# Layer boundaries of a two-block transformer kernel on one core: order of low parts, high parts, squares and additions, and idle matrix products between layers

## The chip, the cores and the metric

The kernel runs on one core of one Trainium2 chip. The metric is the device time of one execution in microseconds (us). The core has five engines that matter here: TensorE (PE) for matrix products, VectorE (DVE), ScalarE (ACT), GpSimd (POOL), and SyncE (SP), which issues the loads. Each engine runs its own list of instructions in order and waits on semaphores that the others raise.

## The reference

The input x is 512 tokens by 1024 features. A first block and then a stack of four mixer layers are applied, every one with a residual and an RMS norm. What matters here is the pattern between two layers:

```
y = xf * lax.rsqrt(jnp.mean(xf * xf, axis=-1, keepdims=True) + EPS)      # rms_norm, times a gain
...
h = h + 0.5 * rms_norm(f, g_ffn1_post[i])
u = rms_norm(h, g_mix_pre[i])
qkv = u @ w_in[i]
...
h = h + rms_norm(mixed @ w_out[i], g_mix_post[i])
f = swiglu(rms_norm(h, g_ffn2_pre[i]), w_ffn2_gate[i], w_ffn2_up[i], w_ffn2_down[i])
h = h + 0.5 * rms_norm(f, g_ffn2_post[i])
e = (p[i] @ w_ple_proj[i]) * jax.nn.sigmoid(h @ w_ple_gate[i])
h = h + rms_norm(e, g_ple_post[i])
```

Four times, then, the output F of a layer is normalized, scaled by a gain and added to h, and the new h is normalized and multiplied by the next layer's weights. All of it is in float32.

## The kernel before

**Layout.** h, F, and the split input of a product are held transposed: 8 blocks (DB = 8) of 128 features by 512 tokens. A float32 product is made of three products of fp32r parts: x is split in a high part xh (ACT) and a low part xl = x − xh (DVE), a weight tile in wh (ACT) and wl (DVE), and TensorE adds xh·wh, xl·wh and xh·wl (`mm3`, lines 320 to 322). A stage of the table `stages` is a row of weight tiles of 1024 by 128; SP loads them four ahead.

**A layer boundary** is what this case is about. At the end of a layer, `post_out` (or the code of the stage ple) squares F block by block on ACT and adds the squares up on POOL (`sum_squares`: a copy for block 0, L459, then additions into `acc`, L462). TensorE sums over the features with products against ones (`sums_pe`, L344: first of `acc`, then of the last square), DVE and ACT make the inverse root, and TensorE spreads it over the partitions (`spread_pe`, L366). Then a new `Block` begins, and `Prologue` runs, with `update` set at four boundaries: into mix_in, ffn2_up, ple and conv_in. Its work for the 8 blocks b is dealt out like this:

- DVE (`Prologue.dve`): F[b] is scaled by the inverse root, read from a PSUM bank, and the gain (L415); for even b the sum h[b] = F[b] + h[b] (L419); the low part xl[b] (L437; L434 in ple, which has no gain), placed two blocks behind the scaling.
- POOL (`Prologue.pool`, `sum_squares`): the sum h[b] for odd b (`add`, L450), and the running sum of the new squares. Before square b is added, for even b, `add(b + 1)` is called.
- ACT (`Prologue.act`): the high part xh[b] (L401), then the square of h[b] into one of two buffers (L405), which from b = 2 on waits until POOL has added square b − 2.
- PE (`pe_tiles`, `head_mm`): the first three tiles of a stage (HEAD = 3) are multiplied together, block by block, so that TensorE can start when block 0 is ready. A block takes six products that need xh[b] (L469, L470) and three that need xl[b] (L473). Behind the head come the sums over squares (`sums_pe`), and, inside the next tile, `spread_pe`.

The stage ple has no squares in its prologue (its input is not normalized); there ACT also copies the products of p and splits weights between the blocks, and DVE splits two weight tiles ahead of its steps 3 and 5. `keep_busy` issues products of constants (ident by ones) whose result nobody reads; before the change it is used around the end of the first block's attention and at the start of mix_out (L1653, L1738, L1749, L1756).

The order within an engine is the order in which the code is written; no scheduler changes it.

Of the kernel before, what the change touches and what calls it, by code (L numbers as in the profile page):

```python
# [29 lines left out]
ACT = mybir.ActivationFunctionType  # L30
# [4 lines left out]
DB = D // P  # L35
# [19 lines left out]
def kernel_program(nc, I, out):  # L55
    top = ExitStack()
    with top:
# [133 lines left out]
        h = sb("h", [P, DB, SEQ])  # L191
# [182 lines left out]
        class Prologue:  # L374
# [17 lines left out]
            def act(self, act, after=()):  # L392

                after = dict(after)
                for b in range(DB):
                    if b in after:
                        after[b](act)
                    if self.update is not None:
                        act.wait_ge(h_pool if b % 2 else h_new, self.h0 + b // 2 + 1)
                    g = 1.0 if self.gain is None else self.gain[:, b:b + 1]  # L400
                    nc.scalar.activation(xh[:, b, :], h[:, b, :], ACT.Copy, scale=g).then_inc(xs_hi, 1)  # L401
                    if self.squares:
                        if b >= 2:
                            act.wait_ge(acc_done, self.acc0 + b - 1)
                        nc.scalar.activation(sq[:, b % 2, :], h[:, b, :], ACT.Square).then_inc(sq_done, 1)  # L405

            def dve(self, dve, after=()):
                after = dict(after)
                for b in range(DB):
                    if b in after:  # L410
                        after[b](dve)
                    if self.update is not None:
                        if b == 0:
                            dve.wait_ge(spread, self.root + 1)
                        nc.vector.scalar_tensor_tensor(out=F[:, b, :], in0=F[:, b, :], scalar=self.update[:, b:b + 1],  # L415
                                                       in1=ps[STAT][:, :], op0=ALU.mult, op1=ALU.mult).then_inc(f_scaled, 1)
                        if b % 2 == 0:
                            dve.wait_ge(f_scaled, self.fs0 + b + 1)
                            nc.vector.tensor_tensor(h[:, b, :], F[:, b, :], h[:, b, :], ALU.add).then_inc(h_new, 1)  # L419
                        if b >= 2:  # L420
                            self.low(dve, b - 2)
                    else:
                        self.low(dve, b)
                if self.update is not None:
                    self.low(dve, DB - 2)
                    self.low(dve, DB - 1)

            def high(self, act, b):
# [23 lines left out]
        def sum_squares(pool, sq0, acc0, add=None):  # L452

            for b in range(DB - 1):
                if add is not None and b % 2 == 0:
                    add(pool, b + 1)
                pool.wait_ge(sq_done, sq0 + b + 1)
                if b == 0:
                    nc.gpsimd.tensor_copy(acc[:, :], sq[:, 0, :]).then_inc(acc_done, 1)  # L459
                else:  # L460
                    pool.wait_ge(acc_done, acc0 + b)
                    nc.gpsimd.tensor_tensor(acc[:, :], acc[:, :], sq[:, b % 2, :], ALU.add).then_inc(acc_done, 1)  # L462
# [33 lines left out]
            return 4 + j if isinstance(i, int) and i == 1 and j < 2 else j  # L496

        def pe_tiles(pe, name, x_hi, x_lo, ev0, x_ready=None, parts=1, sums=None, at=None,
                     beside=None, loop_end=None, x_pe=None, amid=None, bank_of=None, x_at=None, joined=None, frees=False, held=False):

            def body(i, j):
                r, s, kb, t, got = tile_at(name, i, j, 0)
                o, bank, part = output_of(i, j, parts)
                if amid is not None:
                    bank = two_banks(o)  # L510
                if bank_of is not None:
                    bank = bank_of(i, j)
                first_i = isinstance(i, int) and i == 0
                if first_i and x_ready is not None and j < HEAD:
                    if j:
                        return
                    pe.wait_ge(lo_done, t + HEAD)
                    if joined is not None or held:
                        pe.wait_ge(evac, ev0 - 1)
                    for b in range(kb):  # L520
                        if joined is not None and b == 2:
                            sums_pe(pe, *joined)
                        if at is not None and sums is None and b == 4:
                            spread_pe(pe, at)
                        if x_pe is not None:
                            x_pe(pe, b)
                        head_mm(pe, range(HEAD), t, b, x_ready, x_hi, x_lo)
                    if sums is not None:
                        sums_pe(pe, *sums)
                    return  # L530
                pe.wait_ge(lo_done, t + 1)
                if part == 0 and bank < 4:
                    wait(pe, evac, ev0 + o - (3 if amid is None or first_i or o in (4, 5) else 1))
                for b in range(kb):
                    if first_i and j == HEAD and b == 2 and sums is not None:
                        spread_pe(pe, at)
                    xb = part * WB + b
                    if x_at is not None and o == 0 and (b == 0 or xb >= FB - 4):
                        pe.wait_ge(*x_at(max(xb, min(part * WB + kb, FB - 4) - 1)))
                    last = mm3(pe, ps[bank][:, :], s, b, x_hi[:, xb, :], x_lo[:, xb, :],  # L540
                               xb == 0, part == parts - 1 and b == kb - 1)
                    if b == kb - 1:
                        last.then_inc(tile_done, 1)
                    elif frees and o == DB - 1:
                        last.then_inc(x_free, 1)
                    if amid is not None:
                        amid(pe, o, b)
                if beside is not None and isinstance(i, int):
                    beside(pe, 4 * i + j)
            steps(pe, name, body, loop_end, 2 if bank_of is ffn_bank else 1)  # L550


        def in_proj(name, gain, dst, update=None, sums=None, tails=(), evac_dve=None, evac_act=None, loop_end=None,
# [13 lines left out]
            with ExitStack() as own:  # L567
# [81 lines left out]
                @block.tensor  # L649
                def _(pe):  # L650
                    pe_tiles(pe, name, xh, xl, ev0, x_ready=pro.x0, sums=None if joined else pro.sums, at=st, joined=sums,
                             beside=beside.get("pe"), loop_end=loop_end, amid=beside.get("pe_amid"))
                    if "pe" in tails:
                        tails["pe"](pe, ev0)
            return ev0
# [14 lines left out]
        at = 0  # L670
# [113 lines left out]
        def ffn_up(block, name, gain, update, act_hi, act_lo, sp_end=None, boot=None, pool_start=None):  # L784
# [75 lines left out]

            @block.tensor
            def _(pe):
                pe_tiles(pe, name, xh, xl, ev0, x_ready=pro.x0, sums=pro.sums, at=st, bank_of=ffn_bank)
            return ev0


# [5 lines left out]
        def post_out(block, name, x_hi, x_lo, parts=1, x=None, x_at=None, amid=None, between=(None, None)):  # L872
# [51 lines left out]
            @block.tensor  # L924
            def _(pe):
                pe_tiles(pe, name, x_hi, x_lo, ev0, x_ready=x_ready, parts=parts, x_pe=x_pe, x_at=x_at,
                         bank_of=None if x_at is None else down_bank, beside=None if amid is None else amid["pe"])
                sums_pe(pe, acc0 + DB - 1, sq0 + DB, between[0])
                if between[1] is not None:
                    between[1](pe)  # L930
                spread_pe(pe, st)


# [912 lines left out]
        with ExitStack() as c:  # L1846
# [10 lines left out]
            with nc.Block() as block:  # L1857
# [66 lines left out]
                @block.tensor  # L1924
                def _(pe):
                    for o in range(2, DB):
                        p_product(pe, o)
                    t = t0 + PACKED
                    pe.wait_ge(lo_done, t + HEAD)
                    for b in range(DB):  # L1930
                        head_mm(pe, range(HEAD), t, b, pro.x0, xh, xl)
                    for o in range(HEAD, DB):
                        s = (t + o) % SPLIT
                        pe.wait_ge(lo_done, t + o + 1)
                        wait(pe, evac, ev0 + o - 3 if o > 3 else 0)
                        for b in range(DB):
                            last = mm3(pe, ps[o % 4][:, :], s, b, xh[:, b, :], xl[:, b, :], b == 0, b == DB - 1)
                        last.then_inc(tile_done, 1)
                    sums_pe(pe, acc0 + DB - 1, sq0 + DB)
                    spread_pe(pe, st)  # L1940

        ple_ctx.close()

        with ExitStack() as c:
# [14 lines left out]
            with nc.Block() as block:  # L1959
# [64 lines left out]

                @block.tensor
                def _(pe):
                    pe_tiles(pe, name, xh, xl, ev0, x_ready=pro.x0, sums=pro.sums, at=st)

            joint = ExitStack()
            sums, block, pro = resid_out("conv_out", *split_x(lambda b: yall[:, b, :]),  # L2030
# [1121 lines left out]
```

## Time and profile before

| | |
|---|---|
| median of 3 runs | 2263.16 us (2261.5 to 2265.85) |
| the profiled execution's own time | 2260.62 us |
| its span in the trace | 2258.9 us |
| TensorE matmul busy | 2174.8 us, 96% of the span |
| VectorE busy | 1132.9 us, 50% |
| ScalarE busy | 869.1 us, 38% |
| GpSimd busy | 409.6 us, 18% |
| granted TensorE clock, mean | 0.98 of full |
| loads | 182.14 MB, mean 81 GB/s |

Shares are of the whole span. TensorE is nearly always at work, so a time on another engine costs only where TensorE waits for it. Those places are few and short, and the four layer boundaries with an update hold a good part of them. The granted clock is either full (2.4 GHz) or half (1.2 GHz). Starts are in us from the span's start.

### The profile page before, as it was taken

To read this page: it belongs to the slowest core of one execution; us is meant where nothing else is said; L and a number is where in the kernel's file an instruction comes from. 1 tells how busy PE (TensorE), PEld (TensorE's weight loads), DVE (VectorE), ACT (ScalarE), POOL (GpSimd) and SP (SyncE) were. 2 spreads that over 40 slices of the span, in tenths; PEclk is the share of its full clock that TensorE was granted. 3 is DMA by queue.
4 is the path that set the end of the run, shared out by engine and by line. 5 is a ranking of instruction groups with operands and counts; after the bars stand their busy time and mean duration, and the time that the engine had idled before them with its cause. 6 is when DMAs were issued, how large, how long until landed. Compare 5 with 4: busy or idle time off the path is not lost. (4 is left out here: it accounts for less than half of the span.)

```text
span 2258.9 us, 29190 instructions
## 1 busy us (share of the span) xinstructions
PE 2174.8 (96%) x10874; PEld 1760.1 (78%) x10874; DVE 1132.9 (50%) x1801; ACT 869.1 (38%) x1426; POOL 409.6 (18%) x450
## 2 busy tenths in 40 slices
PE   8999999999999999999899999999999999999998
PEld 6888887766677888888778877887788887886667
DVE  5444323544445444322575544336556777665444
ACT  4322223554434322223432233225446753443353
POOL 2111001213313111100230011001110242014441
PEclk9999999999999999999999999999999998999999
DMA  4333333511022333332233346860143221243111
GB/s 144 110 95 100 96 99 84 101 56 56 20 75 57 112 102 93 105 93 76 81 93 102 93 68 96 109 92 20 39 131 89 63 56 39 66 98 75 47 48 47
DMA packets 359323, 182.14 MB, mean 81 GB/s; under 512 B 41925, under 2 KB 356014, under 8 KB 358830
## 3 DMA queue, kind: packets, MB, share of 16 engines
q1 hardware_dynamic: 358872, 180.57, 32.4%
q8 instruction: 69, 1.13, 0.2%
q14 instruction: 40, 0.33, 0.1%
q10 hardware_dynamic: 342, 0.12, 0.0%
HBM read 176.14 MB, written 4.52 MB: 80 GB/s over the span
## 5 line engine op out<-in xcount | busy, mean ns | idle before, releaser
L320 PE MATMUL ps<-xh,wh 128*128 128x512 f32 x1912 | 760.7, 398 | 1.4 <-DVE wl L287 1.4
L322 PE MATMUL ps<-xh,wl 128*128 128x512 f32 x1912 | 745.6, 390 | 0.0
L321 PE MATMUL ps<-xl,wh 128*128 128x512 f32 x1912 | 744.6, 389 | 0.0
L287 DVE TENSOR_TENSOR wl<-raw,wh 128x1024 fp32r<-128x1024 f32 x328 | 417.9, 1274 | 416.4 <-ACT wh L277 412.1
L277 ACT ACTIVATE wh<-raw 128x1024 fp32r<-128x1024 f32 x328 | 341.2, 1043 | 359.2 <-PE ps L322 313.9
L320 PEld LDWEIGHTS ps<-xh,wh 128*128 128x128 f32 x1912 | 359.1, 188 | 83.7 <-issue 10.8
L322 PEld LDWEIGHTS ps<-xh,wl 128*128 128x128 f32 x1912 | 358.9, 188 | 76.6
L321 PEld LDWEIGHTS ps<-xl,wh 128*128 128x128 f32 x1912 | 359.4, 188 | 73.2 <-issue 2.4
L469 PE MATMUL ps<-xh,wh 128*128 128x512 f32 x312 | 129.6, 416 | 25.4 <-DVE wl L287 10.9
L462 POOL TENSOR_TENSOR acc<-acc,sq 128x512 f32<-128x512 f32 x72 | 102.9, 1430 | 263.4 <-ACT sq L904 178.9
L320 PE MATMUL ps<-a_hi,wh 128*128 128x512 f32 x352 | 137.0, 389 | 0.0
L322 PE MATMUL ps<-a_hi,wl 128*128 128x512 f32 x352 | 137.0, 389 | 0.0
L321 PE MATMUL ps<-a_lo,wh 128*128 128x512 f32 x352 | 136.9, 389 | 0.0
L815 POOL TENSOR_TENSOR F<-F,rstd 128x512 f32<-128x512 f32 x44 | 57.1, 1298 | 397.9 <-ACT F L831 397.9
L470 PE MATMUL ps<-xh,wl 128*128 128x512 f32 x312 | 127.0, 407 | 0.0
L473 PE MATMUL ps<-xl,wh 128*128 128x512 f32 x312 | 92.8, 407 | 2.4 <-DVE xl L437 2.4
L469 PEld LDWEIGHTS ps<-xh,wh 128*128 128x128 f32 x312 | 62.2, 199 | 41.7 <-issue 15.5
L834 ACT ACTIVATE a_hi<-ps 128x512 f32 (+1 forms) x44 | 26.3, 598 | 163.3 <-DVE ps L855 163.3
L459 POOL COPY acc<-sq 128x512 f32<-128x512 f32 x12 | 8.9, 739 | 424.1 <-ACT sq L974 318.0
L831 ACT ACTIVATE F<-ps 128x512 f32<-128x512 f32 x44 | 26.3, 599 | 149.6 <-DVE ps L852 149.6
L321 PEld LDWEIGHTS ps<-a_lo,wh 128*128 128x128 f32 x352 | 66.1, 188 | 13.7
L320 PEld LDWEIGHTS ps<-a_hi,wh 128*128 128x128 f32 x352 | 66.1, 188 | 13.7
(397 smaller groups left out, 2564.3 us busy)
## 6 DMA issues: line engine op xcount, KB each, us to landing
raw<-in_w_ffn_gate SPq DMA_DIRECT2D x44, 512.0 KB, 3.8
raw<-in_w_ffn_up SPq DMA_DIRECT2D x44, 512.0 KB, 3.7
raw<-in_w_ffn_down SPq DMA_DIRECT2D x32, 512.0 KB, 3.9
raw<-in_conv_w_in SPq DMA_DIRECT2D x32, 512.0 KB, 4.1
raw<-in_fox_w_in SPq DMA_DIRECT2D x32, 512.0 KB, 10.5
raw<-in_gdn_w_in SPq DMA_DIRECT2D x32, 512.0 KB, 4.1
raw<-in_w_in SPq DMA_DIRECT2D x24, 512.0 KB, 3.8
raw<-in_swa_w_in SPq DMA_DIRECT2D x32, 256.0 KB, 3.8
```

Of the source, the lines that this page charges most:

```text
L277: nc.scalar.activation(wh[s][:, 0:kb, :], raw[r][:, 0:kb, :], ACT.Copy).then_inc(hi_done, 1)
L287: nc.vector.tensor_tensor(wl[s][:, 0:kb, :], raw[r][:, 0:kb, :], wh[s][:, 0:kb, :].bitcast(F32), ALU.subtract).then_inc(lo_done, 1)
L320: pe.matmul(o, wh[s][:, kb, :], x_hi, start=start, stop=False)
L321: pe.matmul(o, wh[s][:, kb, :], x_lo, start=False, stop=False)
L322: return pe.matmul(o, wl[s][:, kb, :], x_hi, start=False, stop=stop)
L462: nc.gpsimd.tensor_tensor(acc[:, :], acc[:, :], sq[:, b % 2, :], ALU.add).then_inc(acc_done, 1)
L469: pe.matmul(ps[g][:, :], wh[s][:, b, :], x_hi[:, b, :], start=b == 0, stop=False)
L470: pe.matmul(ps[g][:, :], wl[s][:, b, :], x_hi[:, b, :], start=False, stop=False)
L473: last = pe.matmul(ps[g][:, :], wh[(t + g) % SPLIT][:, b, :], x_lo[:, b, :], start=False, stop=b == DB - 1)
L815: nc.gpsimd.tensor_tensor(SR[:, s, :], S[:, s, :], rstd[:, :], ALU.mult).then_inc(sr_done, 1)
L831: nc.scalar.activation(S[:, s, :], ps[ffn_bank(i, j)][:, :], ACT.Silu).then_inc(silu_done, 1)
L834: nc.scalar.activation(act_hi[:, bass.ds(p, 1), :], ps[ffn_bank(i, j)][:, :].rearrange("p (o q) -> p o q", o=1), ACT.Copy).then_inc(up_hi, 1)
```

## The change

Five edits:

1. `Prologue.act`: the high part of block b + 1 now comes ahead of the square of block b.
2. `Prologue.dve`: the low part stands one block behind the scaling instead of two.
3. `sum_squares`: POOL's additions to odd blocks of h come ahead of squares 0, 1, 2 and 3, instead of 0, 2, 4 and 6.
4. Idle products: 9 ahead of the head of mix_in, ffn2_up and conv_in (a new argument `idle_bank` of `pe_tiles`), 4 between sums and spread of ffn1_down and mix_out, 8 ahead of the sums of ple and 4 between its sums and spread.
5. ffn2_down, which has products of p between its sums and its spread, gets none; the head of ple gets none either.

```diff
@@ Prologue.act
                     nc.scalar.activation(xh[:, b, :], h[:, b, :], ACT.Copy, scale=g).then_inc(xs_hi, 1)
-                    if self.squares:
-                        if b >= 2:
-                            act.wait_ge(acc_done, self.acc0 + b - 1)
-                        nc.scalar.activation(sq[:, b % 2, :], h[:, b, :], ACT.Square).then_inc(sq_done, 1)
+                    if self.squares and b >= 1:
+                        self.square(act, b - 1)
+                if self.squares:
+                    self.square(act, DB - 1)
+
+            def square(self, act, b):
+                if b >= 2:
+                    act.wait_ge(acc_done, self.acc0 + b - 1)
+                nc.scalar.activation(sq[:, b % 2, :], h[:, b, :], ACT.Square).then_inc(sq_done, 1)
@@ Prologue.dve
-                        if b >= 2:
-                            self.low(dve, b - 2)
+                        if b >= 1:
+                            self.low(dve, b - 1)
                     else:
                         self.low(dve, b)
                 if self.update is not None:
-                    self.low(dve, DB - 2)
                     self.low(dve, DB - 1)
@@ sum_squares
             for b in range(DB - 1):
-                if add is not None and b % 2 == 0:
-                    add(pool, b + 1)
+                if add is not None and b < DB // 2:
+                    add(pool, 2 * b + 1)
                 pool.wait_ge(sq_done, sq0 + b + 1)
@@ pe_tiles
+                    if idle_bank is not None:
+                        keep_busy(pe, idle_bank, 9)
                     pe.wait_ge(lo_done, t + HEAD)
@@ in_proj (mix_in) and ffn_up (ffn2_up); conv_in passes idle_bank=6
+                             idle_bank=None if update is None else 6)
@@ post_out
                 if between[1] is not None:
                     between[1](pe)
+                else:
+                    keep_busy(pe, 6, 4)
                 spread_pe(pe, st)
@@ ple
+                    keep_busy(pe, 4, 8)
                     sums_pe(pe, acc0 + DB - 1, sq0 + DB)
+                    keep_busy(pe, 4, 4)
                     spread_pe(pe, st)
```

**POOL at the start of conv_in.** Names are destination, then sources; `h<-F,h` is the addition to an odd block, `acc<-sq` and `acc<-acc,sq` the running sum of squares. Before:

```order
L450 TENSOR_TENSOR h<-F,h 128x512 [waits f_scaled]
L459 COPY acc<-sq 128x512 [waits sq_done]
L462 TENSOR_TENSOR acc<-acc,sq 128x512 [waits acc_done,sq_done]
L450 TENSOR_TENSOR h<-F,h 128x512 [waits f_scaled]
L462 TENSOR_TENSOR acc<-acc,sq 128x512 [waits acc_done,sq_done] x2
L450 TENSOR_TENSOR h<-F,h 128x512 [waits f_scaled]
L462 TENSOR_TENSOR acc<-acc,sq 128x512 [waits acc_done,sq_done] x2
L450 TENSOR_TENSOR h<-F,h 128x512 [waits f_scaled]
L462 TENSOR_TENSOR acc<-acc,sq 128x512 [waits acc_done,sq_done]
```

Now:

```order
L454 TENSOR_TENSOR h<-F,h 128x512 [waits f_scaled]
L463 COPY acc<-sq 128x512 [waits sq_done]
L454 TENSOR_TENSOR h<-F,h 128x512 [waits f_scaled]
L466 TENSOR_TENSOR acc<-acc,sq 128x512 [waits acc_done,sq_done]
L454 TENSOR_TENSOR h<-F,h 128x512 [waits f_scaled]
L466 TENSOR_TENSOR acc<-acc,sq 128x512 [waits acc_done,sq_done]
L454 TENSOR_TENSOR h<-F,h 128x512 [waits f_scaled]
L466 TENSOR_TENSOR acc<-acc,sq 128x512 [waits acc_done,sq_done] x4
```

Behind the addition to block 7, which waits for DVE's last scaling, there stood one addition of a square; now there stand four.

**ACT at the start of conv_in**, from the high part of block 5 on (`xh<-h,vA`, with its square `sq<-h`). Before:

```order
L401 ACTIVATE xh<-h,vA 128x512 [waits h_new_pool]
L405 ACTIVATE sq<-h 128x512 [waits acc_done]
L401 ACTIVATE xh<-h,vA 128x512 [waits h_new]
L405 ACTIVATE sq<-h 128x512 [waits acc_done]
L401 ACTIVATE xh<-h,vA 128x512 [waits h_new_pool]
L405 ACTIVATE sq<-h 128x512 [waits acc_done]
L277 ACTIVATE wh<-raw 128x1024 [waits tile_done,loaded1]
```

Now:

```order
L401 ACTIVATE xh<-h,vA 128x512 [waits h_new_pool]
L410 ACTIVATE sq<-h 128x512 [waits acc_done]
L401 ACTIVATE xh<-h,vA 128x512 [waits h_new]
L410 ACTIVATE sq<-h 128x512 [waits acc_done]
L401 ACTIVATE xh<-h,vA 128x512 [waits h_new_pool]
L410 ACTIVATE sq<-h 128x512 [waits acc_done] x2
L277 ACTIVATE wh<-raw 128x1024 [waits tile_done,loaded1]
```

The squares between the high parts of blocks 5, 6 and 7 were those of 5 and 6; they are now those of 4 and 5, and the squares of 6 and 7 stand together behind the last high part.

**PE between ple and conv_in** (`ps<-ones,ident` is an idle product) in the kernel after:

```order
L485 MATMUL ps<-ones,ident 128x128 x8
L344 MATMUL ps<-ones,acc 128x1 x4
L344 MATMUL ps<-ones,sq 128x1 x4
L485 MATMUL ps<-ones,ident 128x128 x4
L366 MATMUL ps<-ident,rms_col 128x128 x4
L1867 UNCONDITIONAL_BRANCH
L2037 UNCONDITIONAL_BRANCH
L485 MATMUL ps<-ones,ident 128x128 x9
L473 MATMUL ps<-xh,wh 128x512
```

The three rows of L485 are new; the rest stood there in the same order.

## Rows read from the trace of the kernel before

**Rows 1.** The page, part 1: busy us (share) xinstructions of each engine.

```profile
PE 2174.8 (96%) x10874; PEld 1760.1 (78%) x10874; DVE 1132.9 (50%) x1801; ACT 869.1 (38%) x1426; POOL 409.6 (18%) x450
```

**Rows 2.** Waits of PE, whole span: us in total, times, longest.

```profile
PE ps L469 <- ACT xh L401: 8.1, 3, 2.7
...
PE ps L366 <- ACT rms_col L360: 2.8, 3, 1.0
...
PE ps L344 <- POOL acc L462: 2.5, 1, 2.5
```

**Rows 3.** Stretches: length, busy us (instructions) by engine, granted clock, DMA share, GB/s.

```profile
385.15:409.28 24.13, 21.32 (x89) 17.07 (x90) 21.20 (x21) 10.57 (x17) 17.61 (x13) 0.86 0.62 110
694.76:718.90 24.14, 20.48 (x89) 16.19 (x90) 21.21 (x21) 10.56 (x17) 16.98 (x11) 0.89 0.30 79
1133.93:1158.01 24.08, 21.03 (x89) 16.55 (x90) 21.19 (x21) 10.57 (x17) 17.06 (x13) 0.86 0.29 76
...
1130.40:1140.60 10.20, 6.60 (x20) 4.92 (x21) 7.11 (x12) 3.83 (x7) 4.26 (x6) 0.50 0.58 151
1140.60:1156.10 15.50, 14.82 (x64) 11.57 (x63) 14.59 (x14) 6.95 (x11) 12.84 (x8) 1.00 0.01 2
...
sum 23.80, PE 16.28 PEld 11.83 DVE 19.31 ACT 10.74 POOL 12.66; mean PE 5.43 PEld 3.94 DVE 6.44 ACT 3.58 POOL 4.22
```

**Rows 4.** DVE in order of time, conv_in: start, us, instruction [idle before <-releaser].

```profile
1133.93 0.75 DVE L415 SCALAR_TENSOR_TENSOR F<-F,vA,ps 128x512 f32<-128x512 f32 x1 [1.73 <-PEq L1857]
...
1149.10 0.73 DVE L415 SCALAR_TENSOR_TENSOR F<-F,vA,ps 128x512 f32<-128x512 f32 x1
...
1152.82 1.46 DVE L437 SCALAR_TENSOR_TENSOR xl<-h,vA,xh 128x512 fp32r<-128x512 f32 x1 [0.24 <-ACT xh L401]
...
1158.05 0.16 DVE L351 TENSOR_SCALAR rms_col<-ps 128x4 f32<-128x4 f32 x1 [2.43 <-PE ps L344]
```

**Rows 5.** Line L437, the low parts: duration in ns, min/median/max.

```profile
L437 DVE SCALAR_TENSOR_TENSOR xl<-h,vA,xh x56: 733/1092/1790, 17.8 to 2012.8; 128x512 fp32r<-128x512 f32 x56
```

**Rows 6.** POOL in order of time, conv_in.

```profile
1136.14 1.27 POOL L450 TENSOR_TENSOR h<-F,h 128x512 f32<-128x512 f32 x1 [2.11 <-DVE F L415]
...
1150.29 1.74 POOL L450 TENSOR_TENSOR h<-F,h 128x512 f32<-128x512 f32 x1
1151.98 1.75 POOL L462 TENSOR_TENSOR acc<-acc,sq 128x512 f32<-128x512 f32 x1
```

**Rows 7.** ACT in order of time, conv_in.

```profile
1152.06 0.73 ACT L401 ACTIVATE xh<-h,vA 128x512 fp32r<-128x512 f32 x1 [2.72 <-POOL h L450]
1152.69 0.61 ACT L405 ACTIVATE sq<-h 128x512 f32<-128x512 f32 x1
```

**Rows 8.** PE in order of time, conv_in, low products of block 4.

```profile
1149.23 0.97 PE L473 MATMUL ps<-xl,wh 128*128 128x512 f32 x3 [0.68 <-DVE xl L437]
```

**Rows 9.** PE in order of time, sums and spreads, at three layer ends.

```profile
384.17 0.65 PE L366 MATMUL ps<-ident,rms_col 128*128 128x128 f32 x4 [0.95 <-ACT rms_col L360]
...
693.37 1.06 PE L366 MATMUL ps<-ident,rms_col 128*128 128x128 f32 x4 [0.90 <-ACT rms_col L360]
...
1129.12 1.05 PE L344 MATMUL ps<-ones,acc 128*128 128x1 f32 x8 [2.55 <-POOL acc L462]
1130.03 1.56 PE L344 MATMUL ps<-ones,sq 128*128 128x1 f32 x8
1132.49 1.11 PE L366 MATMUL ps<-ident,rms_col 128*128 128x128 f32 x4 [0.90 <-ACT rms_col L360]
```

**Rows 10.** PE in order of time: idle products that the kernel has already (two records each).

```profile
618.14 1.91 PE L481 MATMUL ps<-ones,ident 128*128 128x128 f32 x8
...
635.82 2.94 PE L481 MATMUL ps<-ones,ident 128*128 128x128 f32 x24
```

**Rows 11.** DVE and PE in order of time, start of ple.

```profile
1079.83 1.22 DVE L287 TENSOR_TENSOR wl<-raw,wh 128x1024 fp32r<-128x1024 f32 x1 [0.56 <-ACT wh L277]
...
1081.11 0.50 PE L469 MATMUL ps<-xh,wh 128*128 128x512 f32 x1 [3.40 <-DVE wl L287]
```

More of the change, by code:

```diff
@@ L498, in pe_tiles @@
         def pe_tiles(pe, name, x_hi, x_lo, ev0, x_ready=None, parts=1, sums=None, at=None,
-                     beside=None, loop_end=None, x_pe=None, amid=None, bank_of=None, x_at=None, joined=None, frees=False, held=False):
+                     beside=None, loop_end=None, x_pe=None, amid=None, bank_of=None, x_at=None, joined=None, frees=False, held=False, idle_bank=None):
             def body(i, j):
@@ L651, in _ @@
                     pe_tiles(pe, name, xh, xl, ev0, x_ready=pro.x0, sums=None if joined else pro.sums, at=st, joined=sums,
-                             beside=beside.get("pe"), loop_end=loop_end, amid=beside.get("pe_amid"))
+                             beside=beside.get("pe"), loop_end=loop_end, amid=beside.get("pe_amid"),
+                             idle_bank=None if update is None else 6)
                     if "pe" in tails:
@@ L862, in _ @@
             def _(pe):
-                pe_tiles(pe, name, xh, xl, ev0, x_ready=pro.x0, sums=pro.sums, at=st, bank_of=ffn_bank)
+                pe_tiles(pe, name, xh, xl, ev0, x_ready=pro.x0, sums=pro.sums, at=st, bank_of=ffn_bank,
+                         idle_bank=None if update is None else 6)
             return ev0
@@ L2026, in _ @@
                 def _(pe):
-                    pe_tiles(pe, name, xh, xl, ev0, x_ready=pro.x0, sums=pro.sums, at=st)
+                    pe_tiles(pe, name, xh, xl, ev0, x_ready=pro.x0, sums=pro.sums, at=st, idle_bank=6)
             joint = ExitStack()
```

## The prediction

> **What bounds the kernel.** I read the page's busy times first. TensorE has 96% of the span and VectorE 50% [rows 1], so only what TensorE waits for can be won. The waits of PE come second. At the layer changes it waits 8.1 us for the first high part (three times 2.7), 2.8 us for the inverse root, 2.5 us for ple's last sum of squares [rows 2]. Third, the stretches: from DVE's first scaling to the end of the sums over the new squares, the three changes with squares (mix_in, ffn2_up, conv_in) take 24.13, 24.14 and 24.08 us [rows 3]. They agree to 0.06 us, though their clocks differ (0.86, 0.89, 0.86) and one has DMA traffic twice as dense as the others. Something that is neither clock nor DMA sets them. In the same rows DVE is busy 21.2 of 24.1 us and POOL 17.
>
> **Who sets the head.** On conv_in, in order of time. After TensorE got the full clock back at about 1140.6, it still waited 0.68 us for the low part of block 4 [rows 8]. From there on it is paced by itself: 64 products in 14.82 us busy, 0.23 us each [rows 3], nine to a block, 2.07 us; at half clock I take 0.42 (idle products go from 0.12 to 0.21 a record [rows 10]). So the supply from DVE sets the first half. DVE's low part takes 0.73 us at least, 1.09 in the middle and 1.79 at most for the same shape [rows 5]; POOL's additions take 1.27 or 1.74 and 1.75 [rows 6]. The pairs fit one at a time: POOL's sum ends at 1153.73, the low part that began at 1152.82 ends 0.55 later [rows 4, 6]. So I let an addition of POOL hold up to 1.16 us and a low part or addition of DVE 0.56 us of a resource that one of the two has at a time (1.74 is 1.27 plus most of a DVE hold; 1.46 is 0.91 of waiting plus 0.55). The scaling, which reads PSUM, stays at 0.73 to 0.75 and needs none of it. The Trainium skill says the same in "SBUF — State Buffer", section "SBUF: two separate sides": the pair of ports of VectorE and GpSimd is an exclusive lock, taken by VectorE when both inputs are in SBUF.
>
> **Edits 1 to 3, one head with squares.** I work it forward on conv_in, in us from the first scaling at 1133.93.
> - Before: the last scaling ends at 15.90 (1149.83), POOL's addition to block 7 at 18.1, high part 7 at 18.86, last sum of squares at 19.80, low part 7 at 20.35, and PE ends its sums at 24.1 [rows 4, 6, 7]. The sums take 2.0 us, so PE asks for POOL's last sum at about 22.1, 2.3 us after it is there.
> - Now DVE has one low part more ahead of the last scaling: 0.73 less 0.07 of overlap, so 16.6. The bound above is a low part at 1.79: 17.6. The bound below is a gain: ahead of that scaling POOL now does 6 instructions instead of 9, three sums less; if one to two of these holds (1.16 each) leave DVE's path net of the extra low part, 14.7. I take 16.6, since the low parts of odd blocks now follow POOL's addition and ACT's high part closely, and DVE will wait for them about as long as it stops waiting for the port.
> - POOL's addition to block 7 ends 1.5 later (between 1.27 and 1.74): 18.1. Then the sum of square 3, 1.6: 19.7. **The new wait is here:** ACT's square 5 waits for that sum (two buffers), and high part 7 is queued behind square 5. Square 5 0.61, high part 0.73: 21.0, where it was 18.86 [rows 7]. PE, which waits for it, does nine products: 23.2. DVE makes low part 7 by 21.8, in time, so low parts are no longer late but the last high part is.
> - POOL has three more sums: 21.0, 22.8 (it meets low part 7), 24.2. `sums_pe` is first in PE's list behind the head and waits for it. The two rounds of sums take 2.0 us (1.05 and as much, less overlap, as in [rows 9] at full clock): 26.2.
> - That is 2.1 us more than 24.1, for each of three: **+6.3 us.** Queued behind square 7 on ACT, and then on DVE, is the split of the next weight tile, which SP's next load waits for. Square 7 follows the sum of square 5 at 22.8; with 0.61 for it and 1.2 for each half of the split [rows 7, 11] the tile is ready at 25.8, 0.4 ahead of PE's need. That covers it; if the cover goes, each us late is a us lost.
>
> **Edit 2 in ple.** Here there are no squares. Two extra low parts stand ahead of the two weight splits, 0.68 each, but DVE idles 0.56 there for ACT anyway [rows 11]. The rest, 0.1, delays the first product of the head, for which PE waits 3.40 already: **+0.1 us.**
>
> **Edit 4.** An idle product is two records; 24 took 2.94 us at full clock, 8 took 1.91 at half [rows 10], so 0.12 and 0.21 a record.
> - Room: 4 of them are 8 records, 0.96 us, in gaps of 0.90 to 0.95 ahead of the spreads [rows 9]; some hundredths. 9 are 2.1 us in a pause of 2.7 [rows 2]; 8 are 1.9 in the 2.55 ahead of ple's sums. At full clock nothing is delayed. At half clock 9 would be 3.8 us and start the head 1.1 late.
> - Gain: the spread takes 0.65 at full clock and 1.06 and 1.11 at half, and ple's second sums 1.56 against 1.05 [rows 9]. If the clock stays up, that is 0.4 at ffn2_up, and 0.5 + 0.4 at conv_in: **−1.3 us.** Mix_in's spread had full clock already.
> - The half clock in the heads themselves is worth nothing in the sum, as PE caught up with DVE's supply in spite of it [rows 3, 8].
> - The half-clock stretches of the three changes add up to 23.8 us [rows 3]. The Trainium skill, "TensorE: Matmul & The Clock Gate", section "Terms", counts a stretch at half clock as costing half of its length; by that the idle products would return 11.9 us where the sum has 1.3. The trace disagrees for the heads: the three changes took the same time with stretches of 6.8, 6.8 and 10.2 us.
>
> **Sum.** 6.3 + 0.1 − 1.3 = +5.1 us: 2265.7 against the profiled execution's 2260.62. That one was 2.5 below the median of 2263.16, so I forecast 2268.3 us. A measurement of this kernel tells about 0.2% (4.5 us) from no change.
>
> **The rivals.**
> 1. *POOL's late sums set the end (forecast), 50%.* +5.1, from 3 to 7: a quarter of it is under 4.5, as the step of 2.1 may be 1.5.
> 2. *The port frees, 27%.* Fewer sums ahead of the last scaling let it end at 14.7; the whole tail moves up 1.9, and a head costs 0.2: 0.6 + 0.1 − 1.3 = −0.6, so 2262.6. For it: DVE is busy 21.2 of 24.1 us [rows 3], and its low parts take 1.09 to 1.79 where 0.73 would do [rows 5]. Against: ACT's idle time of 2.72 ahead of odd high parts [rows 7] shows that path has little to give.
> 3. *Faster, PE sets its own pace, 10%.* One mechanism: lows and highs arrive before PE asks, from the first block on. Then a head ends 2.35 + 8 × 2.07 after the first scaling and the sums at 21.0, 3.1 earlier, at three heads: −9.3 + 0.1 − 1.3 = −10.5, 2252.7. It decides where the last scaling ends: the tail behind it is 9.6 us, so to gain 4.5 in all, 1.1 a head, it must end by 13.4, and 11.4 gives the full gain. Counted from the clock instead, 23.8 us at 0.42 a product instead of 0.23 are 10.8 us, nearly the same 2252.4: PE would have to be the bound all through. By the rule of the Trainium skill's page "TensorE: Matmul & The Clock Gate" above it would be 2251.3.
> 4. *The idle products don't hold the clock, or the new waits lower it again, 13%.* The new waits (some 1.8 us for high part 7, 1.0 for the last sum) stand where PE was dense before. If half of a stretch as short as before's (6.8 us) falls on dense products behind them, at 0.42 instead of 0.23 each, a head costs some 1.6 more, with nothing to hide it: up to +4.8, 2273.1. It is also the case where the change doesn't do what it says. Against: the same idle products kept the clock full around mix_out's start.
>
> **How the numbers follow.** Slower by over 4.5: three quarters of case 1 and all of case 4, with rounding 0.53. Same: the rest of case 1 and most of case 2, 0.34. Faster: case 3 and a sliver of 2, 0.13. The range leaves out case 3 and the worst of 4: 2260.5 to 2272.5. Case 1 alone has 2266 to 2270.5.
>
> **What the profile will show.** If right: the three stretches from first scaling to the sums' end are 25.5 to 26.7 us; PE has a new wait for POOL's sum (L344 on L466) three times of about 1 us, and for the last high part of about 1.8; spreads take 0.65 everywhere; clock near 1.0 in the heads; low parts of blocks 0 to 2 come sooner. Wrong, if the last scaling ends before 15.5 us or the sums find POOL done.

## The result and the profile after

| | before | after |
|---|---|---|
| median | 2262.11 us (8 runs, 2261.19 to 2268.88) | 2273.86 us (8 runs, 2267.73 to 2278.83) |
| ratio after / before | | 1.005, 95% interval 1.0038 to 1.0063 |
| profiled execution: its time, its span | 2260.62, 2258.9 | 2274.41, 2272.7 |

The change makes the kernel 11.75 us slower. The forecast was 5.1 us, and its range ended at 2272.5 us. The direction is right; the size is not, and the measured time lies above the range.

The page after, part 1, against [rows 1]:

```profile
PE 2189.1 (96%) x10968; PEld 1769.2 (78%) x10968; DVE 1127.1 (50%) x1801; ACT 870.6 (38%) x1426; POOL 408.0 (18%) x450
```

TensorE is busy 14 us longer for 94 more records, which cannot fill more than some 11 us at 0.12 each. The other engines have the same counts as before. DVE and POOL are busy a little less (5.8 and 1.6 us), ACT 1.5 us more; nothing was added there.

The waits of PE after, whole span, against [rows 2]:

```profile
PE ps L473 <- ACT xh L401: 5.4, 8, 1.4
...
PE ps L344 <- POOL acc L466: 3.1, 3, 1.3
...
PE ps L485 <- PEq L1867: 0.3, 1, 0.3
```

The three waits of 2.7 us for the first high part are filled with idle products. In their place PE now waits up to 1.4 us for the last high part, and up to 1.3 for POOL's last sum.

The three stretches from the first scaling to the sums' end, columns as in [rows 3]:

```profile
385.76:412.32 26.56, 24.25 (x107) 17.92 (x108) 19.65 (x21) 11.02 (x17) 16.82 (x13) 0.94 0.52 90
695.64:722.83 27.19, 23.53 (x107) 17.45 (x108) 19.55 (x21) 11.02 (x17) 16.36 (x11) 0.97 0.23 59
1141.98:1168.21 26.23, 23.25 (x107) 18.08 (x108) 19.55 (x21) 11.02 (x17) 16.45 (x13) 0.95 0.23 61
```

The stretches of 24.1 us are now 26.2 to 27.2 us long, although the clock in them went up: it was 0.86 to 0.89 and is 0.94 to 0.97. DVE, busy 21.2 us of them before, is now busy 19.6 and idle the rest.

In order of time, conv_in after, first scaling at 1141.98; DVE, then ACT, POOL and PE, against [rows 4, 6, 7]:

```profile
1157.76 0.73 DVE L420 SCALAR_TENSOR_TENSOR F<-F,vA,ps 128x512 f32<-128x512 f32 x1
1158.60 1.81 DVE L441 SCALAR_TENSOR_TENSOR xl<-h,vA,xh 128x512 fp32r<-128x512 f32 x1
1162.86 0.75 DVE L441 SCALAR_TENSOR_TENSOR xl<-h,vA,xh 128x512 fp32r<-128x512 f32 x1 [2.45 <-ACT xh L401]
```

```profile
1161.59 0.63 ACT L410 ACTIVATE sq<-h 128x512 f32<-128x512 f32 x1 [3.02 <-POOL acc L466]
1162.12 0.71 ACT L401 ACTIVATE xh<-h,vA 128x512 fp32r<-128x512 f32 x1
```

```profile
1158.57 1.29 POOL L454 TENSOR_TENSOR h<-F,h 128x512 f32<-128x512 f32 x1 [1.28 <-DVE F L420]
1159.82 6.35 POOL L466 TENSOR_TENSOR acc<-acc,sq 128x512 f32<-128x512 f32 x4
```

```profile
1162.88 0.50 PE L473 MATMUL ps<-xh,wh 128*128 128x512 f32 x1 [1.45 <-ACT xh L401]
...
1166.23 1.05 PE L344 MATMUL ps<-ones,acc 128*128 128x1 f32 x8 [1.00 <-POOL acc L466]
```

This is the chain of the prediction. POOL's addition to block 7 waits for the last scaling (1158.49), four sums follow it (6.35 us), square 5 waits 3.02 us on ACT for the first of them with high part 7 behind it, and PE waits for both ends.

What the prediction's sum left out stands behind the heads. These are the stretches that begin at the sums' end, ffn2_up and conv_in, first after and then before:

```profile
722.90:732.00 9.10, 9.10 (x32) 7.33 (x33) 3.85 (x7) 3.42 (x5) 1.30 (x1) 0.71 0.19 55
1168.30:1175.00 6.70, 6.70 (x26) 5.42 (x26) 3.84 (x8) 4.33 (x5) 0.00 (x0) 0.75 0.29 78
```

```profile
719.00:728.00 9.00, 8.50 (x39) 6.69 (x39) 4.84 (x9) 4.58 (x6) 1.29 (x1) 1.00 0.22 63
1158.10:1165.00 6.90, 6.90 (x33) 5.69 (x33) 5.38 (x10) 4.34 (x5) 0.00 (x0) 1.00 0.24 70
```

Before, TensorE has the full clock there. After, it has half clock for a part of it, and 6 to 7 products fewer fit, at 0.23 us each: some 1.4 to 1.7 us each time.

**Where the time went.** I took the end of each of the 328 weight splits on DVE in both profiled executions and their difference, place by place. Growth across each boundary, in us:

| | after − before | forecast |
|---|---|---|
| into mix_in | +2.4 | +2.1 |
| into ffn2_up | +4.3 | +1.7 |
| into ple | +1.7 | +0.1 |
| into conv_in | +4.2 | +1.2 |
| the rest (start, attention, last two layers) | +1.2 | 0 |
| sum of the two traces' weight splits | +13.8 | +5.1 |

The rest is made of steps of −1.6 to +2.4 at places that the change does not touch, and the two largest go with stretches at half clock. Ahead of mix_out (−1.6) the trace before has two of 3.4 us and the one after has one. In the last two layers (+2.4) the trace before has stretches of 23.9 and 3.4 us, the one after of 27.3 and 6.8; runs 2 and 9 below have the longer pair and the same step (+3.1 and +2.6), run 11 the shorter pair and no step. So single executions of one kernel differ by such steps.

### The profile page after: what moved, and what is told of

Its sections match the earlier page's. It is cut to its first block and busy times, and to the rows that moved or that the text cites. A ratio compares the mean times of both kernels' runs of the same rounds, so it can differ in the third digit from the quotient of the medians.

```text
span 2272.7 us, 29378 instructions
## 1 busy us (share of the span) xinstructions
PE 2189.1 (96%) x10968; PEld 1769.2 (78%) x10968; DVE 1127.1 (50%) x1801; ACT 870.6 (38%) x1426; POOL 408.0 (18%) x450
## 5 line engine op out<-in xcount | busy, mean ns | idle before, releaser
L320 PEld LDWEIGHTS ps<-a_hi,wh 128*128 128x128 f32 x352 | 66.1, 188 | 13.8
```

What stands on the lines that cost most here:

```text
L320: pe.matmul(o, wh[s][:, kb, :], x_hi, start=start, stop=False)
```

## The experiments

All edits are against the kernel before unless said otherwise. "Stretch" is from the first scaling to the sums' end.

**1. The reorder without idle products** (edits 1 to 3; their diff is above).

> Edits 1 to 3, no new idle products. Late-sums theory (the new order of POOL's and ACT's work ends a head later, and the idle products only add to it): the stretch from DVE's first scaling to the end of the sums is 26.1 to 26.6 us at mix_in, ffn2_up and conv_in, as in the changed kernel, against 24.1 before; PE's first product 2.4 us after the scaling everywhere; the time is +6 to +8 us against the kernel before. Clock theory (idle products at half clock make the loss): about +1 us, and the stretches are near 24.1.

Measured: 2278.33 us against 2261.26, ratio 1.0075 (1.006 to 1.0089). The stretches are near the 26.1 to 26.6 expected, ffn2_up's 0.8 above; the loss of 17 us is more than twice the 6 to 8 us expected from the late sums. The three stretches, and what follows each:

```profile
387.08:413.81 26.73, 22.23 (x89) 17.88 (x90) 19.62 (x22) 11.01 (x17) 16.81 (x13) 0.82 0.60 89
704.68:732.08 27.40, 22.55 (x89) 18.27 (x90) 19.56 (x21) 11.00 (x17) 16.37 (x11) 0.81 0.23 61
1150.40:1176.67 26.27, 21.26 (x89) 16.38 (x90) 19.58 (x22) 11.01 (x17) 16.50 (x13) 0.88 0.24 61
412.80:419.40 6.60, 6.60 (x21) 5.43 (x22) 2.52 (x7) 3.05 (x4) 0.00 (x0) 0.50 0.54 120
730.20:736.80 6.60, 6.60 (x23) 5.62 (x24) 1.77 (x6) 1.49 (x2) 0.00 (x0) 0.50 0.27 79
1177.30:1180.50 3.20, 3.20 (x11) 2.61 (x10) 0.81 (x2) 3.18 (x5) 0.00 (x0) 0.50 0.57 163
```

The order alone makes the stretches of the changed kernel, so the late sums are its work and not the idle products'. TensorE is at half clock a second time, behind each head, busy all through: 21 and 23 products in 6.6 us where 29 would fit. In this profile the four boundaries grow by 16.1 us together.

**2. The idle products without the reorder.**

```diff
+                    if idle_bank is not None:
+                        keep_busy(pe, idle_bank, 9)
...
+                else:
+                    keep_busy(pe, 6, 4)
...
+                    keep_busy(pe, 4, 8)
                     sums_pe(pe, acc0 + DB - 1, sq0 + DB)
+                    keep_busy(pe, 4, 4)
```

> Edit 4 alone, the old order. Late-sums theory: stretches 24.1 at all three heads; ffn2_up's first scaling comes 0.4 us earlier, conv_in's up to 0.7 later where the idle products run at half clock; in all -1 to +1 us. Clock theory: the half clock that fell on the old pauses now falls on dense products behind the heads, +3 to +6 us.

Measured: 2260.98 against 2261.26, ratio 1.0001 (0.9989 to 1.0013).

```profile
384.65:408.80 24.15, 21.46 (x107) 17.32 (x108) 21.21 (x21) 10.57 (x17) 17.62 (x13) 1.00 0.63 112
693.81:717.95 24.14, 21.44 (x107) 17.32 (x108) 21.22 (x21) 10.56 (x17) 16.99 (x11) 1.00 0.30 79
1132.87:1157.01 24.14, 21.41 (x107) 17.32 (x108) 21.23 (x21) 10.57 (x17) 17.10 (x13) 1.00 0.30 76
```

The clock is full through all three heads, and the stretches are 24.14 as at 0.86: the half clock in the old heads cost nothing. By the weight splits ffn2_up gains 0.43 us and conv_in 0.95, the two terms of the forecast (0.4 and 0.9). They don't show in the median. In the same profile ple loses 0.9 us, where its head has half clock for 6.8 us instead of 3.4, and the last layers lose the 3.1 us named above; an execution varies by more than the two gains.

**3. POOL's sums cut short.** The additions of squares in the three prologues take 8 of 512 columns, which leaves out most of the sum there (`width` is 8 in them; the cut lines pass it on).

```diff
-nc.gpsimd.tensor_tensor(acc[:, :], acc[:, :], sq[:, b % 2, :], ALU.add)
+nc.gpsimd.tensor_tensor(acc[:, 0:width], acc[:, 0:width], sq[:, b % 2, 0:width], ALU.add)
```

> The kernel before, but POOL's six additions of squares in the prologues into mix_in, ffn2_up and conv_in take 8 columns instead of 512, so most of the sum of squares is left out there. Shared-resource theory (POOL and DVE one at a time, an addition of POOL holding 1.16 us): DVE's low parts fall to 0.74 to 1.3 us, the last scaling ends about 13.1 us after the first instead of 15.9, and the stretch falls to 22.2 (to 23.5 at half clock), set by PE. Rival (DVE's low part simply takes 1.1 to 1.8 us here): the last scaling still ends at 15.9 and the stretch stays at 24.1.

Measured: one time, 2258.66. Line L437, then DVE in conv_in (first scaling at 1132.05), against [rows 4, 5]:

```profile
L437 DVE SCALAR_TENSOR_TENSOR xl<-h,vA,xh x56: 734/741/1790, 18.3 to 2010.8; 128x512 fp32r<-128x512 f32 x56
```

```profile
1144.40 0.73 DVE L415 SCALAR_TENSOR_TENSOR F<-F,vA,ps 128x512 f32<-128x512 f32 x1
...
1147.73 0.75 DVE L437 SCALAR_TENSOR_TENSOR xl<-h,vA,xh 128x512 fp32r<-128x512 f32 x1 [0.24 <-ACT xh L401]
```

The median low part falls from 1.09 to 0.74 us, though nothing in DVE's own work changed, and the last scaling ends 13.08 us after the first (15.9 before, 13.1 expected). What lengthens DVE's instructions is POOL's work beside them. The stretches are 22.7 to 23.6 us (22.2 to 23.5 expected).

**4 to 7. The edits one by one,** one timed execution each. First edit 2:

> Edit 2 alone (low part one block behind the scaling, ple too). Late-sums theory, worked forward with one holder at a time: last scaling ends near 17.4 instead of 15.9, stretch 24.6 us against 24.1. Rival (an earlier low part helps, PE had been waiting for it): 23 to 24.

Edit 3:

> Edit 3 alone (odd additions ahead of squares 0 to 3). Late-sums theory: POOL stands still for the last two scalings and has four sums behind the last addition; last scaling near 15.1, stretch 25.7. Rival (additions early are good for PE, harmless for the sums): 24.1 or less.

Edit 1:

> Edit 1 alone (high part of the next block ahead of the square). Late-sums theory: each square waits for the next block's h, so POOL's sums start late: last scaling near 14.8, stretch 25.9. Rival (high parts come earlier, harmless): 24.1 or less.

Edits 1 and 3:

> Edits 1 and 3, low parts two behind as before. Late-sums theory: the two fit each other (POOL does the next odd addition while the square is not there yet), so less than either alone: stretch 24.9, last scaling near 14.8. If the costs simply added up: 27.5.

| | last scaling ends | stretch, three heads | expected | time of the one run (before 2258.17) |
|---|---|---|---|---|
| edit 2, low | 17.6 | 24.66, 24.70, 24.67 | 24.6 | 2261.84 |
| edit 3, adds | 15.1 | 25.63, 25.61, 25.68 | 25.7 | 2269.04 |
| edit 1, high | 14.9 | 25.87, 25.87, 25.88 | 25.9 | 2273.18 |
| edits 1 and 3 | 14.8 | 24.95, 25.26, 24.98 | 24.9 | 2269.14 |

These come from a forward working of the three queues, DVE, ACT and POOL, with one holder at a time (0.56 us for DVE's sums and low parts, 1.16 for POOL's additions). It met every stretch within 0.1 us but one (25.26); edit 2's last scaling was expected at 17.4. By the stretches not one of the edits helps by itself, and edits 1 and 3 together cost less than each alone. The times don't rank them: each is a single execution, and the 3.7 to 15 us over the kernel before are more than their three stretches add up to (1.7 to 5.3 us). In edit 1's profile POOL stands still for squares that ACT now makes late (conv_in):

```profile
1159.70 3.03 POOL L467 TENSOR_TENSOR acc<-acc,sq 128x512 f32<-128x512 f32 x2 [1.35 <-ACT sq L410]
1162.69 1.29 POOL L455 TENSOR_TENSOR h<-F,h 128x512 f32<-128x512 f32 x1
1165.33 1.35 POOL L467 TENSOR_TENSOR acc<-acc,sq 128x512 f32<-128x512 f32 x1 [1.35 <-ACT sq L410]
```

With edits 1 and 3 together PE waits 1.0 to 1.3 us for POOL's last sum at all three heads, and 0.4 us or less for the last high part. Behind two of the heads half clock follows. Ffn2_up's wait, and what comes behind its sums:

```profile
PE ps L344 <- POOL acc L467: 1.3, 1, 1.3
...
722.50:726.00 3.50, 3.50 (x12) 2.81 (x11) 0.78 (x3) 1.49 (x2) 0.00 (x0) 0.51 0.51 150
```

With edit 3 or edit 1 alone PE waits 1.2 to 1.5 us for the last high part and not for the sum, and there is no half clock behind any head.

In ple the first product of the head comes 12.34 us after the first scaling with edit 2 alone and 11.84 without it: 0.5, not the 0.1 of the forecast. There the first low part, now early, meets POOL's first addition, which takes 1.81 instead of 1.29, and ACT's chain to the weight split follows it.

**8. A worked-out order.** The same forward working, run over many orders; for the three heads with squares, no new idle products.

```diff
+ACT:  "x0 s0 x1 s1 x2 x3 s2 x4 s3 x5 s4 s5 x6 s6 x7 s7"        (x high part, s square)
+DVE:  "f0 f1 h0 f2 h2 l0 f3 l1 f4 l2 h4 l3 f5 l4 f6 h6 l5 f7 l6 l7"   (f scaling, h sum, l low part)
-                if add is not None and b % 2 == 0:
-                    add(pool, b + 1)
+                if add is not None and b in (0, 2, 3, 5):
+                    add(pool, {0: 1, 2: 3, 3: 5, 5: 7}[b])
```

> An order worked out with the one-at-a-time rule, no new idle products: POOL's additions to odd blocks ahead of squares 0, 2, 3 and 5; DVE scales blocks 0 and 1 first and then has its low parts one to two behind; ACT makes high parts 2 and 3 before square 2 and 4 before square 3, and squares 4 and 5 together ahead of high part 6. Late-sums theory: last scaling ends at 15.0, POOL's last sum at 19.5 to 20, stretch 22.2 at full clock and 23.2 where the first 7 us of the head are at half clock; -2 to -5 us in all. Rival (order is worth nothing, port time is all): 24.1 and no difference.

Measured: 2257.79 against 2261.26, ratio 0.9984 (0.9975 to 0.9994). The gain of 3.5 us is the expected one, and its interval does not reach 1. The last scaling ends at 15.1, POOL's last sum at 20.3 (19.5 to 20 expected). The stretches are 23.40, 23.77 and 22.83 at clocks of 0.82 to 0.86, up to 0.6 above the 23.2 expected where the head begins at half clock.

**9. The changed kernel with idle products in its new gaps.**

```diff
+                        if idle_bank is not None and b == kb - 1:
+                            keep_busy(pe, idle_bank, 5)
                         head_mm(pe, range(HEAD), t, b, x_ready, x_hi, x_lo)
                     if sums is not None:
+                        if idle_bank is not None:
+                            keep_busy(pe, idle_bank, 4)
                         sums_pe(pe, *sums)
```

> The changed kernel, with 5 more idle products where PE waits for the last high part of a head and 4 where it waits for POOL's last sum (1.2 and 1.0 us, inside waits of 1.4 and 1.0 to 1.3). Clock-behind-the-head theory: the stretches stay at 26.2, but the half clock that followed the heads on dense products is gone or rarer, and the time falls 3 to 6 us under the changed kernel's, to +5 to +8 over the kernel before. Rival (the late sums alone make the loss, the clock is luck): no difference from the changed kernel within 2 us.

Measured: 2268.01 against 2261.62, ratio 1.0038 (1.0025 to 1.005). The stretches, and what follows conv_in's:

```profile
385.63:411.88 26.25, 24.88 (x125) 19.09 (x126) 19.61 (x22) 11.02 (x17) 16.81 (x13) 1.00 0.59 91
695.17:721.72 26.55, 24.89 (x125) 19.09 (x126) 19.57 (x21) 11.01 (x17) 16.38 (x11) 1.00 0.23 61
1137.00:1163.26 26.26, 24.89 (x125) 19.09 (x126) 19.57 (x21) 11.01 (x17) 16.48 (x13) 1.00 0.23 61
1163.30:1175.00 11.70, 11.70 (x54) 9.64 (x54) 10.05 (x16) 4.34 (x5) 0.00 (x0) 1.00 0.47 134
```

Full clock in the heads and behind them, as expected. The stretches stay long, and by the weight splits the boundaries grow by 2.05 (mix_in), 1.93 (ffn2_up) and 1.16 us (conv_in) over the kernel before: the forecast's 2.1, 1.7 and 1.2. Ple keeps +1.3. The time is 3.5 us under run 11's, but the six and the five executions overlap (2267.26 to 2276.3, and 2268.66 to 2276.24), so the medians alone don't show that the filled waits help; the profiles do.

**10. The worked-out order with the idle products of edit 4.**

> The worked-out order together with the idle products of edit 4. Full clock in the heads, where PE and not DVE is now the bound: stretch 22.2 at all three, first scaling 0.4 earlier at ffn2_up and 0.9 at conv_in: -6 to -8 us against the kernel before. Rival (idle products are worth nothing, as in their run alone): -3.5, as the order alone.

Measured: 2254.94 against 2261.62, ratio 0.996 (0.9947 to 0.9973), the fastest of all kernels here.

```profile
385.86:408.16 22.30, 21.25 (x107) 17.31 (x108) 17.98 (x21) 10.82 (x17) 17.91 (x13) 1.00 0.64 107
695.78:718.13 22.35, 21.33 (x107) 17.32 (x108) 17.99 (x22) 10.82 (x17) 16.35 (x11) 1.00 0.27 71
1132.24:1154.58 22.34, 22.18 (x107) 18.45 (x108) 18.00 (x21) 10.82 (x17) 16.72 (x13) 0.94 0.27 71
```

22.3 us at all three heads (22.2 expected). Idle products that are worth nothing measurable in the old order, where DVE sets the head, take another 0.5 to 1.4 us off each stretch in this one (23.40, 23.77 and 22.83 without them). Here PE and not DVE sets the head's end: from DVE's last scaling to the sums PE has no wait over 0.2 us. Ahead of conv_in the idle products did not hold the clock: it fell for 3.4 us in the spread, which took 0.86 us, and the first product came 3.2 us after the scaling instead of 2.9.

**11. The changed kernel once more.**

> The changed kernel once more, on the same chip as the two others: +11 to +12 us, stretches 26.2 to 27.2; if the half clock behind the heads is a matter of luck, it falls on other heads than in the first profile.

Measured: 2271.53 against 2261.62, ratio 1.0044 (1.0031 to 1.0057): +9.9 us, a little less than expected. Stretches of half clock behind the heads and around ple's end:

```profile
413.20:416.40 3.20, 3.20 (x11) 2.59 (x10) 0.31 (x2) 2.82 (x4) 0.00 (x0) 0.50 0.88 215
723.70:730.30 6.60, 6.60 (x21) 5.53 (x22) 1.89 (x5) 1.72 (x3) 0.00 (x0) 0.50 0.27 79
1140.10:1146.80 6.70, 6.38 (x29) 6.00 (x30) 2.95 (x7) 0.93 (x2) 0.54 (x3) 0.50 0.16 47
1170.90:1174.10 3.20, 3.20 (x11) 2.61 (x10) 0.57 (x2) 3.06 (x5) 0.00 (x0) 0.50 0.57 164
```

Half clock behind ffn2_up's and conv_in's heads and over ple's end came in both profiles of the changed kernel; behind mix_in's head it came in this one alone. Ahead of conv_in PE started the head 0.9 us late in both. The 4 idle products between ple's sums and spread, in the changed kernel's first profile and then in run 2:

```profile
1138.75 2.06 PE L485 MATMUL ps<-ones,ident 128*128 128x128 f32 x8
...
1130.85 1.14 PE L481 MATMUL ps<-ones,ident 128*128 128x128 f32 x8
```

In the first profile mix_in's half clock came 5 us before the sums' end instead, so that PE reached the sums late and had no wait for POOL there.

It is not mere luck. The 13 profiles of this case have 39 heads with squares. In 11 of them PE waits 1.0 to 1.3 us for POOL's last sum: three each in runs 1, 7 and 11, two in the changed kernel's first profile. Half clock begins within 2 us of the sums' end in 10 of these 11, and in none of the other 28. The eleventh is run 7's conv_in.

## Why the prediction was right or wrong

- **What sets the head: right, and shown.** Runs 2 and 3 separate it: full clock leaves the stretch at 24.14, and taking POOL's work away shortens DVE's low parts to 0.74 and the stretch to 22.7 to 23.6. That POOL and DVE hold something one at a time was argued from pairs of rows. Run 3 shows that POOL's work is the cause, and six orders worked with this rule came out within 0.4 us (the changed order in run 9, runs 4 to 7, and the worked-out order in run 10). By the Trainium skill's page "SBUF — State Buffer", section "SBUF: two separate sides", a VectorE instruction with two inputs in SBUF and a GpSimd instruction that reads SBUF take turns on a shared pair of ports, each for its whole length. The runs agree that they take turns (0.74 us without POOL's additions beside, 1.09 with them); they fit with holds a little shorter than the instructions (0.56 of 0.73 us, 1.16 of 1.27).
- **Edits 1 to 3, +2.1 a head: right.** Step by step: last scaling 16.6 (16.5 measured), addition to block 7 18.1 (17.9), high part 7 21.0 (20.9), last sum 24.2 (24.2), sums' end 26.2 (26.2 to 27.2). The new wait for the last high part is 1.4 us, where 1.8 was forecast. Ffn2_up's 27.2 has half clock in its sums (0.6), and POOL's last sum 0.3 later.
- **Ple, +0.1: wrong by a small sum.** It costs 0.5 by order; the idle time of DVE that I counted as cover moved along with ACT's chain. The rest of ple's 1.7 goes with a half-clock stretch of 6.8 us instead of 3.4 in its head; run 2, with the old order and the same 6.8, loses 0.9 there.
- **Edit 4, −1.3: right where the clock stays up** (runs 2 and 9: 0.43 at ffn2_up; 0.95 at conv_in). In the changed kernel ffn2_up's 0.4 came, conv_in's 0.9 did not: the clock fell over ple's sums in spite of 8 idle products ahead of them. The 4 behind the sums then took 2.06 us, where in run 2 they took 1.14 (the estimate was 0.96), and held up the spread, and conv_in's first scaling came 0.7 later instead of 0.9 earlier.
- **The step that failed is "Sum".** It adds 6.3, 0.1 and −1.3, and puts the clock behind the new waits at nothing. Rival 4 ("the new waits lower it again") was given 13% and up to +4.8, but the forecast's own wait for POOL's last sum brings it about, as the count in run 11 shows. In the profiles the boundaries grow by 12.6 us where the sum has 5.1. Of the 7.5 between them, 3.1 are half clock on products behind the heads of ffn2_up and conv_in (1.7 and 1.4), 1.6 are conv_in's late start, 1.6 are ple (0.4 by order, the rest half clock), 0.9 is ffn2_up's stretch, and 0.3 mix_in's. Run 9 fills the waits at the heads, and its boundaries grow by 6.4 us (its clock also stayed up over ple's end, which its edit does not touch). By medians it loses 6.4 us against the kernel before; the changed kernel loses 9.9 on the same chip, and 11.75 in its first measurement. I had priced the clock in the heads rightly as worth nothing, and overlooked that the new waits put it where PE has work.
- **Near rival 4 by luck, in part.** With its +4.8 the time would have been 2273.1, and 2273.86 was measured. But it priced three heads at 1.6, while in the profile two heads paid that, and ple and conv_in's start, which it did not price, paid the rest.
- **The rivals.** "The port frees" is out: fewer of POOL's sums ahead of the last scaling did not bring it earlier (16.5). DVE is busy 15.8 us up to there, as before, with one low part more: what the port gave back went into that low part, and 0.6 us of new waits for high parts came on top. In runs 5 to 7, without edit 2, the last scaling does come at 14.8 to 15.1, and the stretch is long all the same. "Faster, PE sets its own pace" is out for this order; run 10 comes near that case by another order (22.3 us a head, where the rival had 21.0).
- **The range** ended at 2272.5 because I cut the upper end of rival 4 with it. The chances have a slip too: three quarters of case 1 and all of case 4 are 0.505, not 0.53.
- **Open:** why the 8 idle products ahead of ple's sums hold the clock up to conv_in's head in runs 2 and 9 and not in the changed kernel's two profiles, nor quite in run 10. The same instructions stand 3 to 10 us later in the changed kernel's traces than in those of runs 2 and 9; no run here tells whether that is the reason. What sets the lengths of the half-clock stretches in ple's head and in the last layers is open as well.

## What to carry to other kernels

Work a boundary of several in-order engines forward by hand, with every wait and what is queued behind it, before moving one instruction earlier: here each "earlier" pushed the running sum towards the end, where TensorE needs it. Two engines that share something slow each other, so order their work in turn, and ask which sum ends last rather than which part starts first. And price a new wait on TensorE twice: once for its length, once for the dense products behind it that may run at half clock.

## What the runs showed of the hardware that was not expected

- A wait of 1.0 to 1.3 us followed by 2 us of one-column sums was followed by half clock at 10 of 11 heads, with a wait of 1.4 us for the last high part ahead of it or, in run 7, with 0.4 us or less. A wait for the last high part alone, of 1.2 to 1.5 us, was followed by none in runs 5 and 6, and by 3.4 us, over before the sums' end, at mix_in in the changed kernel's first profile. With both waits filled by idle products half clock did not come behind a head (run 9).
- Idle products are no cure that always holds: 1.95 us of them ahead of ple's sums kept the clock in runs 2 and 9, and not in the two profiles of the changed kernel. At half clock 8 records took 2.06 us where they took 1.14 at full clock, and so delayed what they should protect.
- The same reordering costs 17 us without idle products and 10 to 12 with them, though the idle products alone are worth nothing in the old order. So the effects of the edits don't add up.
